# Feed-forward down products two blocks behind the up products, with every block turned by VectorE

## The reference

```
x = x + jnp.square(jax.nn.relu(h2 @ w_ff1[i])) @ w_ff2[i]        # first block, 4096 wide

def swiglu(x, w_gate, w_up, w_down):                             # second block, 2816 wide
    return (jax.nn.silu(x @ w_gate) * (x @ w_up)) @ w_down
x = x + FFN_RES * swiglu(rms_norm_2(x, ffn1_norm[l]), ...)       # ahead of the attentions
x = x + FFN_RES * swiglu(rms_norm_2(x, ffn2_norm[l]), ...)       # behind them
```

## Time and profile before

| | us |
|---|---|
| median of 3 runs | 974.15 |
| lowest, highest | 973.94, 974.36 |
| profiled execution | 973.86 |
| its span | 972.0 |

### The profile page before, as it was taken

One profiled execution on the slowest core, in us unless ns is written; L12 is line 12 of the kernel. 1 busy time (PEld: TensorE's weight loads), 2 busy tenths in 40 slices (PEclk: granted clock), 3 DMA queues, 4 the chain that ended last, 5 costly groups with the idle time before them and its releaser, 6 DMA issues.

```text
span 972.0 us, 12800 instructions
## 1 busy us (share of the span) xinstructions
PE 964.7 (99%) x4548; PEld 794.7 (82%) x4548; DVE 742.9 (76%) x1268; ACT 506.5 (52%) x682; POOL 65.7 (7%) x97
## 2 busy tenths in 40 slices
PE   9999999999999999999999999999999999999997
PEld 6877888888888888888888888888887788888886
DVE  6898885478668887885778878786758877878784
ACT  7645555644464444444774444445648664444442
POOL 4101000020020000000120000000203020000000
PEclk9999999999999999999999999999999999999999
DMA  9765455434566555654565656544654255656531
GB/s 347 264 198 158 160 174 180 140 130 173 173 215 214 187 202 185 204 180 168 175 229 185 205 178 206 183 147 137 220 175 151 87 174 176 213 175 211 177 129 44
DMA packets 98724, 175.67 MB, mean 181 GB/s; under 512 B 5920, under 2 KB 54128, under 8 KB 98672
## 3 DMA queue, kind: packets, MB, share of 16 engines
q1 hardware_dynamic: 97024, 171.53, 52.6%
q0 software_dynamic: 1344, 3.19, 1.2%
q10 hardware_dynamic: 304, 0.27, 0.1%
HBM read 173.91 MB, written 1.05 MB: 180 GB/s over the span
## 4 chain that ended last, share of the span: by engine, by line
PE 94%; DVE 4%; POOL 1%; issue 1%; ACT 0%; POOLq 0%; ACTq 0%
PE bank L518 84%; PE bank L532 3%; DVE qaT L1606 1%; DVE w_lo L1540 1%; PE bank L577 1%; PE bank L576 1%; PE bank L809 1%; DVE kaT L1606 1%; PE bank L588 1%; PE bank L948 1%; PE bank L648 0%; POOL g_rows L2210 0%; PE bank L814 0%; PE bank L1010 0%; POOL rs L2194 0%
## 5 line engine op out<-in xcount | busy, mean ns | idle before, releaser
L518 PE MATMUL bank<-w_hi,hA 128*128 128x512 f32 (+1 forms) x1720 | 537.6, 390 | 0.2 <-DVE w_lo L1540 0.2
L1540 DVE TENSOR_TENSOR w_lo<-raw,w_hi 128x2048 fp32r<-128x2048 f32 (+1 forms) x159 | 358.0, 2260 | 94.8 <-ACT w_hi L1085 93.9
L1085 ACT ACTIVATE w_hi<-raw 128x2048 fp32r<-128x2048 f32 (+1 forms) x162 | 306.1, 1894 | 169.3 <-PE bank L518 163.9
L518 PEld LDWEIGHTS bank<-w_hi,hA 128*128 128x128 f32 x1720 | 321.4, 188 | 67.0 <-issue 1.4
L518 PE MATMUL bank<-w_lo,hA 128*128 128x512 f32 (+1 forms) x860 | 328.1, 388 | 0.0
L518 PEld LDWEIGHTS bank<-w_lo,hA 128*128 128x128 f32 x860 | 161.6, 188 | 32.2
L1901 DVE STREAM_TRANSPOSE act_T<-act_f 32x128 f32<-32x128 f32 x288 | 87.1, 302 | 3.7
L518 PE MATMUL bank<-w_hi,fT_hi 128*128 128x512 f32 x232 | 71.8, 391 | 0.0
L518 PE MATMUL bank<-w_hi,fT_lo 128*128 128x512 f32 x232 | 71.5, 389 | 0.0
L518 PE MATMUL bank<-w_lo,fT_hi 128*128 128x512 f32 x232 | 71.5, 389 | 0.0
L1353 ACT ACTIVATE act_r<-bank,rs 128x256 f32<-128x256 f32 x44 | 20.9, 475 | 58.5 <-PE bank L518 56.7
(11 more groups left out here) (296 smaller groups left out, 905.7 us busy)
## 6 DMA issues: line engine op xcount, KB each, us to landing
raw<-in_w_in SPq DMA_DIRECT2D x74, 512.0 KB, 4.5
raw<-in_w_ff SPq DMA_DIRECT2D x64, 512.0 KB, 4.2
raw<-in_ffn_w_gate SPq DMA_DIRECT2D x44, 512.0 KB, 3.9
raw<-in_ffn_w_up SPq DMA_DIRECT2D x44, 512.0 KB, 4.8
raw<-in_ffn_w_down SPq DMA_DIRECT2D x44, 512.0 KB, 4.0
raw<-in_w_out SPq DMA_DIRECT2D x16, 512.0 KB, 4.3
raw<-in_w_branch_diff SPq DMA_DIRECT2D x8, 512.0 KB, 4.0
raw<-in_w_branch_ret SPq DMA_DIRECT2D x8, 512.0 KB, 4.2
```

What stands on the lines that cost most here:

```text
L518: mm = pe.matmul(o, a, w, start=first and t == 0 and m < len(outs), stop=last and t == n - 1 and m >= len(todo) - len(outs))
L1085: act.activation(w_hi[u % HI_SLOTS][:, 0:w], raw[u % RAW_SLOTS][:, 0:w], ACT.Copy).then_inc(hi_ready, 1)
L1540: vec.tensor_tensor(w_lo[u % RAW_SLOTS][:, 0:w], raw[u % RAW_SLOTS][:, 0:w], w_hi[u % HI_SLOTS][:, 0:w].bitcast(f32), ALU.subtract).then_i ...
```

## The change

In all three feed-forwards the down products of block i now come behind the up products of block i + 2: up 0, up 1, up 2, down 0, up 3, down 1, and so on, with the last two down blocks at the end. Units of weights are numbered and loaded in that order. Block 1's up products go to banks 2 and 3 instead of 4 and 5. Every block is turned by VectorE: the transposes of TensorE for the blocks 0 and 10, and the wide form of block 7 in `ff`, are gone. On VectorE the low part of a turned block now comes in the step of the next block.

```
-    up = lambda tb, i=1: bank[4 + tb if i else tb]
+    up = lambda tb, i: bank[2 * min(i, 2) + tb]
...
             for j in range(2):
                 narrow(u + j, w_ff1, 4 * j, 4, i * HALF, HALF, turns)
             for j in range(2):
-                wide(u + 2 + j, w_ff2, i * HALF - HALF + 2 * j * P, turns)
-        ff_step(u + 2, 1)
+                wide(u + 2 + j, w_ff2, i * HALF - 2 * HALF + 2 * j * P, turns)
...
         for i in range(1, last + 1):
-            relu_up(i) if i < last else relu_wide(i)
-            for j in range(2):
-                for tb in range(TB):
-                    mm = relu_down(i - 1, tb, j)
-                mm.then_inc(unit_used, 1)
+            relu_up(i)
+            for d in {1: (), last: (last - 2, last - 1)}.get(i, (i - 2,)):
+                for j in range(2):
+                    for tb in range(TB):
+                        mm = relu_down(d, tb, j)
+                    mm.then_inc(unit_used, 1)
...
             def step(i, r=0):
-                v = u + 2 + 3 * (i - 1)
-                ff_up(v, name, i, base + i, SUB, 12 * r, 4 * r)
+                v = u + 4 + 3 * (i - 2)
+                ff_up(name, v, i, base + i, 12 * r, 4 * r)
                 for tb in range(TB):
-                    if i == 1:
+                    if i == 2:
                         acc_free(name, tb)
-                        pe.wait_ge(up_out, 2 * base + 2)
-                    mm = down(v + 2, i - 1, tb, r, i == 1)
+                        pe.wait_ge(up_out, 2 * base + 2 + 2 * tb)
+                    mm = down(v + 2, i - 2, tb, r, i == 2)
                 mm.then_inc(unit_used, 1)
...
-            v, i = u + 2 + 3 * (n - 2), n - 1
-            pe.wait_ge(up_out, 2 * (base + i))
-            narrow_block(up(0)[:, :], None, v, 0, HALF).then_inc(up_done, 1)
-            narrow_block(up(1)[:, :], None, v, 1, HALF, lambda: ff_turn(name, i, 2 * (base + n), SUB, blocks=(0,)))
-            down(v + 2, i - 1, 0)
-            ff_turn(name, i, 2 * (base + n), SUB, blocks=(1,))
-            down(v + 3, i, 0, last=True).then_inc(acc_done, 1)
+            v, i = u + 31, n - 1
+            down(v, i - 1, 0)
+            down(v + 1, i, 0, last=True).then_inc(acc_done, 1)
...
+            hi(u + 33)
+            act.wait_ge(unit_used, u + 31)
+            turned_split(n - 1)
```

More of the change, by code:

```diff
@@ L1286, in _ @@
         split(("p",))
-        for i in range(1, DFF // HALF):
-            v = U0["ff"] + 2 + 4 * (i - 1)
+        hi(U0["ff"] + 5)
+        relu_split(0)
+        hi(U0["ff"] + 6)
+        for tb in range(TB):
+            relu(1, tb)
+        for i in range(2, DFF // HALF):
+            v = U0["ff"] + 4 * (i - 1)
             hi(v + 3)
-            if i == 1:
-                for tb in range(TB):
-                    split(("ff", 0, tb))
+            relu_split(i - 1)
             hi(v + 4)
-            for b in range(2):
-                relu(i, b) if i < DFF // HALF - 1 else wide_low(i, b)
+            for tb in range(TB):
+                relu(i, tb)
             hi(v + 5)
[L1298 to L1303, removed]
+            hi(v + 6)
+        hi(U0["ff"] + 31)
+        relu_split(DFF // HALF - 1)
+        hi(U0["ff"] + 32)
         def ple_copy(tb):
@@ L1362, in gated @@
             hi(u + 4)
+            hi(u + 5)
+            turned_split(0)
+            hi(u + 6)
+            silu(1, 0)
+            silu(1, 1)
             def step(i, r=0):
-                v = u + 2 + 3 * (i - 1)
+                v = u + 4 + 3 * (i - 2)
+                if i > 2:
+                    hi(v + 2, r)
                 hi(v + 3, r)
[L1367 to L1371, removed]
+                turned_split(i - 1, r)
                 hi(v + 4, r)
@@ L1374, in step @@
                     silu(i, tb, r)
[L1375 to L1376 removed]
+            step(2)
             with act.Fori(0, 2) as r:
[L1378 removed]
+                for i in range(3, 7):
                     step(i, r)
[L1380 to L1388 removed]
+            hi(u + 33)
+            act.wait_ge(unit_used, u + 31)
+            turned_split(n - 1)
+            hi(u + 34)
         gated("f1", "ffn1", DFF // HALF)
@@ L1912, in gated @@
             lo(u + 4)
+            turn_act(0)
+            lo(u + 5)
+            turned_low(0)
+            lo(u + 6)
+            multiply(1, 0)
+            multiply(1, 1)
             def step(i, r=0):
-                v = u + 2 + 3 * (i - 1)
-                if i > 1:
-                    turn_act(i - 1, r)
+                v = u + 4 + 3 * (i - 2)
+                turn_act(i - 1, r)
+                if i > 2:
+                    lo(v + 2, 12 * r)
                 lo(v + 3, 12 * r)
-                if i == 1:
-                    for tb in range(TB):
-                        split((name, 0, tb))
-                else:
-                    turned_low(i - 1, r)
+                turned_low(i - 1, r)
                 lo(v + 4, 12 * r)
@@ L1926, in step @@
                     multiply(i, tb, r)
-                lo(v + 5, 12 * r)
-            step(1)
+            step(2)
             with vec.Fori(0, 2) as r:
-                for i in range(2, 6):
+                for i in range(3, 7):
                     step(i, r)
-            v, i = u + 2 + 3 * (n - 2), n - 1
-            turn_act(i - 1)
-            turned_low(i - 1)
-            multiply(i, 0)
-            lo(v + 3)
-            split((name, i, 0))
-            lo(v + 4)
-            multiply(i, 1)
-            split((name, i, 1))
-            lo(v + 5)
+            turn_act(n - 1)
+            turned_low(n - 1)
+            lo(u + 33)
             if norm_out == "final":
```

191 lines of the change are left out of this document (66 added, 125 removed).

## The result

| | us |
|---|---|
| before, median of 6 runs | 974.18 (973.94 to 974.86) |
| after, median of 6 runs | 979.84 (978.33 to 981.41) |
| after over before | 1.0059, 95% interval 1.0048 to 1.0070 |
| profiled execution after, its span | 979.68, 977.9 |

The change makes the kernel slower by 5.7 us. The executions of after also lie 3 us apart, where those of before lie within 1.

What follows compares the result with a forecast made beforehand. The prediction took TensorE, which works without holes in the feed-forwards, as the bound: 974.15 us, -3.25 spared, +3.4 and +3.1 for two waits, gives 977.4; one clock fall of 1.6 makes 979.0, range 975.5 to 981.0.

Steps and rivals of the forecast that it cites:

- The bound and the gain: All feed-forwards: TensorE runs without a hole, so the spared transposes and block 7's wide form gain 3.25 us in full.
- The first wait: First feed-forward, unit 9: TensorE waits for VectorE's low part, queued behind block 2's turn; costs 3.4 us.
- Unit 7, just in time: First feed-forward: VectorE completes unit 7's low part at 320.02, TensorE wants it at 320.11; no wait.
- The second wait: Second feed-forward, block 3's up products: TensorE waits for block 2's first multiply on VectorE; 2.99 + 0.08 = 3.1 us.
- The third feed-forward: Its start: VectorE is earlier here, its list ends at 823.16, wanted at 823.66; no wait, 0.4 us to spare.
- The ends: Block 10 of gated feed-forwards: VectorE's 7.7 us hides under 8.2 us of down products; otherwise each costs up to 1.
- The sum without the clock: Whole kernel: the gain and both waits change 974.15 by +3.2 us to 977.4; chance 0.25 that the clock stays.
- The clock: TensorE's clock can fall behind the two holes; 0 to 1.6 us per fall, one taken, giving 979.0, chance 0.35.
- The case with two falls: Both waits come and TensorE's clock falls behind both: 980.6 us, chance 0.15.
- the likeliest: Whole kernel: both waits come and the clock falls behind one of them, 977.4 + 1.6 = 979.0 us, chance 0.35.
- No wait at all: Rival: VectorE goes through its list before TensorE asks, only the spared 3.25 us count: 970.9 us, chance 0.10.
- One wait only: Rival: VectorE finds 3 us in one feed-forward, so only one wait comes: 974.2 us, chance 0.08.

Runs made afterwards that it cites:

- fix_both: Changed kernel with VectorE's order altered at both waits, and ScalarE's in the gated feed-forwards, nothing added or removed: 970.93 us, ratio 0.9968 to before.
- fill12: Changed kernel with 12 more products that nobody reads on TensorE just ahead of each of the two waits: 976.95 us, ratio 1.0028 to before.
- fill6: Changed kernel with 6 more products that nobody reads on TensorE just ahead of each of the two waits: 977.00 us, ratio 1.0031 to before.
- fix_ff: Changed kernel with VectorE reordered only in the first feed-forward, low parts of units 9 and 10 ahead of block 2's turn: 975.44 us, ratio 1.0013 to before.
- fix_gated: Changed kernel with VectorE and ScalarE reordered only in the gated feed-forwards, block 2's multiplies and silus earlier: 975.79 us, ratio 1.0016 to before.
- block0: Changed kernel with block 0 of each feed-forward turned by TensorE again, VectorE's order otherwise not repaired: 972.73 us, ratio 0.9985 to before.
- fill3: Changed kernel with 3 more products that nobody reads on TensorE just ahead of each of the two waits: median 977.12 us, ratio 1.0035 to before.

## Why the prediction was right, and where it was off

**The bound and the gain held.** TensorE had no slack; what it was spared came back in full. Forecast 3.25; the three feed-forwards of fix_both are 1.15, 0.78 and 1.02 us shorter than before, 2.95 in all, with some 0.3 us of small waits left in them. The third feed-forward of after, where nothing waited, gained 1.01 of 1.01.

**The first wait.** Forecast at unit 9, from 330.99 to 334.27 and 0.08 for starting up; measured 3.00. VectorE's list was right to 0.1 us over 38 us (the low part complete at 333.97, with a start of after 0.08 earlier, against 334.13). The forecast hole of 3.28 was 0.28 too long: TensorE asked 0.12 later than forecast, mostly by what unit 7 lost, the low part was 0.08 earlier, and TensorE started 0.06 behind its end where 0.14 was taken.

**Unit 7, just in time.** It was forecast to be in time by 0.09, and lost 0.1: the down products of block 0 take from 314.59 to 325.58, 10.99 instead of 10.88.

**The second wait.** Forecast 2.99, measured 2.95. **The third feed-forward.** Forecast none with 0.4 to spare; none came. **The ends.** Hidden, as forecast.

**The sum without the clock.** Forecast 977.4; fill12 and fill6, which pay the waits and have no fall, are 976.95 and 977.00. The forecast was 0.4 too high; some 0.3 of it is the first wait.

**The clock: mechanism right, size off.** The step that was mis-sized is "I take 1.6 and one fall of the two possible". A fall costs 1.60 and 1.30 in the profiled execution of after, at or under the 1.6. But both waits brought one there, and the fastest execution of after, 978.33, is already 1.4 above fill12. On the median the falls cost 2.9 us, nearly two. The case with two falls, 980.6 at 0.15, was nearer than the likeliest at 979.0, and the measured time lies between them, inside the range. Part of the closeness is luck: the forecast had the time without a fall 0.4 us too high and the falls 1.3 too cheap (1.6 against 2.9), which cancel in part. The slowest execution, 981.41, is 4.5 above fill12, more than two falls of 1.6; its mean granted clock, 0.994, is the lowest, and what happened in it stays open.

Two readings of the clock need a word. The price was taken from the pitch of the first products (0.43); the granted clock doesn't show it there (it reads 1.00 from 1.40 to 4.60 in before). The stretches above have both, 0.43 at 0.50, and bear the price out. And the forecast looked for a clock below 1 in a slice; no slice of the page shows it, only the short stretches do.

**The rivals.** No wait at all (970.9) isn't what the change does, but it is what the same instructions do in another order: fix_both gave it to 0.1 us. One wait only (974.2, and with the clock 975.7) is what fix_ff and fix_gated showed. The rule on transposes of the Trainium skill, page "VectorE: DVE Perf Modes", section "Rules for kernel authors", gives the right choice for block 0 in this order (block0 beats after), and the wrong one once VectorE's order is repaired (fix_both beats block0 by 1.8).

## What to carry to other kernels

An engine with a quarter of its time free can still be late: walk its list from the last place where it was idle, with start-to-start times from the trace, and compare with the time at which the bound engine asks. When work moves to such an engine, put what the bound engine asks for next ahead of what only has to be done some time; here that turned +5.7 us into -3.2. And a wait of 2 to 3 us on TensorE can bring a fall of its clock, which cost 1.3 to 1.6 us more in the traces here, and which no slice of the page shows: a spread of the runs is the sign to look for.

## What the runs showed of the hardware

- A hole of 3.0 us in TensorE's work brought its clock to half for 3.4 us (0.50 in the stretches above), and the fall can come after work has begun again: 0.25 us after it here, over 1 us after in fill3. With two holes of 2.2 us it happened in two of five executions, with two of 1.5 in none of six (one execution of each is traced, the others are judged by their times). The Trainium skill, page "TensorE: Matmul & The Clock Gate", section "Part 1: The HAM clock gate (the "warmup" mystery)", has the fall behind idle time and the return after sustained work; the traces agree.
- The same instructions spread over 0.5 us without such holes (fix_both) and over 3 with two of them (after).
- A product of 128x512 takes 0.43 us, start to start, at a granted clock of 0.50 and 0.227 at 1.00; the low clock after one hole made a feed-forward 1.3 to 1.6 us longer.
- Twelve products that nobody needs, in each of the two holes, made the kernel 2.9 us faster.
